# Values of the second block's attention made as channels by tokens, with four transposes in each layer

## The reference, cut to what matters

```python
h = modulate(rms_norm_2(x, norm_mix[l]), sh1, sc1)
hc = modulate(rms_norm_2(xc, norm_mix[l]), csh1, csc1)
k, v, q, u, f, gt = jnp.split(h @ w_in[l], IN_SPLITS, axis=-1)
if last:
    kc, vc = jnp.split(hc @ w_in[l][:, :2 * KV_WIDTH], 2, axis=-1)
else:
    kc, vc, qc, uc, fc, gtc = jnp.split(hc @ w_in[l], IN_SPLITS, axis=-1)
...
o = latent_attention(q, k, v, kc, vc, attn_sink[l])
...
o = (jnp.einsum('bhgnqk,bnkhd->bnqhgd', p_lat, vb)
     + jnp.einsum('bhgnqc,bchd->bnqhgd', p_ctx, vc))
```

## Time and profile before

| | us |
|---|---|
| median of three runs | 2189.99 |
| lowest, highest | 2189.62, 2190.36 |
| the profiled execution, its own time | 2188.52 |
| its span in the trace | 2186.8 |
| TensorE busy in the span | 2085.0 |
| VectorE, ScalarE, GpSimd busy | 1230.1, 1112.0, 959.3 |
| mean granted TensorE clock | 0.98 of full speed |

### The profile page before, as it was taken

The page is one execution under the profiler, slowest core; times in us unless marked ns, Lnnn a source line. Parts: engine busy times, 40 slices in busy tenths (PEclk is TensorE's granted clock), DMA queues, the critical chain, the costliest instruction groups (busy, mean ns, idle before and its releaser), DMA issues.

```text
span 2186.8 us, 36805 instructions
## 1 busy us (share of the span) xinstructions
PE 2085.0 (95%) x14870; PEld 1856.7 (85%) x14870; DVE 1230.1 (56%) x2034; ACT 1112.0 (51%) x1892; POOL 959.3 (44%) x424
## 2 busy tenths in 40 slices
PE   6999999999999999999999999999999989999997
PEld 6998998998898999988666876778888777898997
DVE  5577757345677655473464435455544546766565
ACT  5575476544585475554475233433333346645553
POOL 4655654653546555642112332323333233465662
PEclk9999999999999999999999999999999989999998
DMA  6454544565654544563212434333333333354551
GB/s 238 150 189 170 185 149 147 183 221 186 225 177 157 182 155 154 195 227 110 97 68 77 163 127 164 116 125 125 116 135 107 131 109 109 124 183 140 189 184 58
DMA packets 93321, 330.65 MB, mean 151 GB/s; under 512 B 10080, under 2 KB 13408, under 8 KB 92896
## 3 DMA queue, kind: packets, MB, share of 16 engines
q1 hardware_dynamic: 93152, 328.30, 43.6%
HBM read 327.08 MB, written 1.18 MB: 150 GB/s over the span
## 4 chain that ended last, share of the span: by engine, by line
PE 76%; DVE 11%; ACT 7%; issue 2%; DMA 2%; POOL 2%; SPq 0%; DVEq 0%; ACTq 0%; POOLq 0%
PE ps L878 21%; PE ps L879 21%; PE ps L880 21%; ACT t_hi L1239 2%; PE ps L932 2%; DVE t_lo L1554 1%; DMA t_A<-cu_scratch 1%; PE ps L891 1%; PE ps L892 1%; PE ps L893 1%; POOL t_lo L2021 1%; PE ps L1150 1%; DVE t_SQA L1564 1%; PE ps L1006 1%; PE ps L1160 1%
## 5 line engine op out<-in xcount | busy, mean ns | idle before, releaser
L2021 POOL TENSOR_TENSOR t_lo<-t_raw,t_hi 128x1024 fp32r<-128x1024 f32 (+1 forms) x360 | 884.9, 2468 | 1059.7 <-ACT t_hi L1239 1035.9
L878 PE MATMUL ps<-t_RB,t_hi 128*128 128x256 f32 (+1 forms) x3712 | 1170.8, 315 | 17.3 <-DVE t_RB L1842 5.3
L879 PE MATMUL ps<-t_RB,t_hi 128*128 128x256 f32 (+1 forms) x3712 | 1149.4, 310 | 0.0
L880 PE MATMUL ps<-t_RB,t_lo 128*128 128x256 f32 (+1 forms) x3712 | 1148.7, 309 | 0.0
L878 PEld LDWEIGHTS ps<-t_RB,t_hi 128*128 128x128 f32 x3712 | 712.3, 192 | 90.5 <-issue 31.5
L880 PEld LDWEIGHTS ps<-t_RB,t_lo 128*128 128x128 f32 x3712 | 712.6, 192 | 35.7
L879 PEld LDWEIGHTS ps<-t_RB,t_hi 128*128 128x128 f32 x3712 | 712.9, 192 | 34.9 <-issue 1.9
L1239 ACT ACTIVATE t_hi<-t_raw 128x1024 fp32r<-128x1024 f32 (+1 forms) x506 | 524.7, 1042 | 421.6 <-PE ps L880 387.9
L1554 DVE TENSOR_TENSOR t_lo<-t_raw,t_hi 128x1024 fp32r<-128x1024 f32 x146 | 211.2, 1447 | 264.4 <-ACT t_hi L1239 264.3
L1980 DVE SCALAR_TENSOR_TENSOR t_A<-ps,t_V,t_A 128x510 f32<-128x510 f32 (+1 forms) x176 | 102.2, 612 | 153.8 <-ACT t_A L1514 152.2
L1514 ACT ACTIVATE t_A<-ps,t_V 128x512 f32<-128x512 f32 (+1 forms) x88 | 48.5, 576 | 126.8 <-PE ps L880 126.8
(11 more groups left out here) (295 smaller groups left out, 2154.5 us busy)
## 6 DMA issues: line engine op xcount, KB each, us to landing
t_raw<-in_W SPq DMA_DIRECT2D x586, 512.0 KB, 3.5
t_A<-cu_scratch SPq DMA_DIRECT2D x8, 512.0 KB, 6.3
t_B<-cu_scratch SPq DMA_DIRECT2D x8, 512.0 KB, 4.4
t_raw<-in_W SPq DMA_DIRECT2D x16, 256.0 KB, 2.6
t_A<-in_C SPq DMA_DIRECT2D x2, 1536.0 KB, 6.8
t_X<-in_X SPq DMA_DIRECT2D x2, 512.0 KB, 4.4
t_X<-in_X SPq DMA_DIRECT2D x1, 1024.0 KB, 9.6
out<-t_X SPq DMA_DIRECT2D x1, 1024.0 KB, 4.8
```

The costliest lines, as they stand in the source:

```text
L878: mm(o, hi[:, w], xh(k), start=k == 0 and j == 0, stop=False)
L879: mm(o, hi[:, w], xl(k), start=False, stop=False)
L880: i = mm(o, lo[:, w], xh(k), start=False, stop=k == nkt - 1 and m == u.x[1] - 1)
L2021: tt(t.lo[s][:, 0:w], t.raw[r][:, 0:w], t.hi[s][:, 0:w].bitcast(F), ALU.subtract).then_inc(*up("pool", ("split", u.i)))
```

## The change

`v2` becomes a copy of `k2` on weight columns 128 to 255: the weight is stationary and 512 tokens stream past it, 24 matmuls in a layer. The result lies as channels by tokens. ScalarE copies it to `VR`, 512 columns in the constants' tile `C1` that no longer hold constants in use. One tick later than the one behind `v2`, a new unit `v2t` turns it: TensorE transposes four blocks of 128 by 128 into one of the small PSUM banks, and ScalarE copies this bank into `V2`. The waits of `pair4` are the same.

```diff
@@ block2
         self.add("v2", l=l, i=i, g=(self.bank(),))
         self.split_after(i, 1)
+        self.v2_turn(l)
         self.tick()
...
+    def v2_turn(self, l):
+        def g():
+            yield
+            self.add("v2t", l=l, s=(self.sbank(),))
+        self.side.append(g())
@@ Tiles
+        self.VR = self.C1[:, CONST["swap1"][0] + 512:CONST["swap1"][0] + 1024]
@@ tensor
     def v2(u):
-        toks(u, 8, 256, 128, 128, block(t.H2), block(t.HL2), (0, 1, 2, 3), lambda k: at("h", 3 + 2 * u.l, k), 1)
+        b, (xh, xl) = gbank(u), h2(512)
+        for k in range(8):
+            q.wait_ge(at("h", 3 + 2 * u.l, k))
+            hi, lo = weights(u, k, 256)
+            o = by_stream(b[:, :])
+            mm(o, hi[:, 128:256], xh(k), start=k == 0, stop=False)
+            mm(o, hi[:, 128:256], xl(k), start=False, stop=False)
+            i = mm(o, lo[:, 128:256], xh(k), start=False, stop=k == 7)
+            taken(u, i, k, 8, 256, ("mm", u.i, 1))
+
+    def v2t(u):
+        q.wait_ge(at("v2raw", u.l))
+        b = sbank(u)
+        for n in range(4):
+            i = e.transpose(b[:, n * 128:(n + 1) * 128], t.VR[:, n * 128:(n + 1) * 128], t.ident)
+        i.then_inc(*up("pe", ("v2tr", u.l)))
@@ scalar
     def v2(u):
-        act(t.V2[:, :, :], gbank(u, 1)[:, :].rearrange("p (b c) -> p b c", b=4), ACT.Copy).then_inc(
-            *up("act", ("v2", u.l), ("gfree", u.g[0])))
+        act(t.VR, gbank(u, 1)[:, :], ACT.Copy).then_inc(*up("act", ("v2raw", u.l), ("gfree", u.g[0])))
+
+    def v2t(u):
+        q.wait_ge(at("v2tr", u.l))
+        act(t.V2[:, :, :], t.sb[u.s[0] % 4][:, :].rearrange("p (b c) -> p b c", b=4), ACT.Copy).then_inc(
+            *up("act", ("v2", u.l), ("sfree", u.s[0])))
```

More of the change, by code:

```diff
@@ L1197, in tensor @@
                 small=small, small4=small4, vc=vc, vb=vc, scores=scores, turn=turn, pv=pv, ssm0=ssm0, ssm3=ssm3, ssm4=ssm4,
-                rope2=rope2, gn_sum=gn_sum, proj=proj, wout=wout, uf=uf, k2=k2, v2=v2, q2=lambda u: of_h2(u, 256 if u.l else 512),
+                rope2=rope2, gn_sum=gn_sum, proj=proj, wout=wout, uf=uf, k2=k2, v2=v2, v2t=v2t, q2=lambda u: of_h2(u, 256 if u.l else 512),
                 gate2=lambda u: of_h2(u, u.x[3]), rope2b=rope2b, pool1=pool1, four1=four1, mix2=mix2, pair0=pair0, pair3=pair3,
@@ L1529, in scalar @@
                 small1=small1, small2=small2, exp=exp, turn=turn, pv=pv, ssm0=ssm0, ssm1=ssm1, ssm3=ssm3, z=z, ysplit=ysplit,
-                gate=gate, gn_sum=gn_sum, gn_sqrt=gn_sqrt, msplit=msplit, rope=rope, norm2=norm2, uf=uf, mix2=mix2, k2=k2, v2=v2,
+                gate=gate, gn_sum=gn_sum, gn_sqrt=gn_sqrt, msplit=msplit, rope=rope, norm2=norm2, uf=uf, mix2=mix2, k2=k2, v2=v2, v2t=v2t,
                 q2=q2, pair1=pair1, pair3=pair3, pair4=pair4, gate2=gate2, msplit2=msplit2, up=ffup, glu=glu)
```

## The result

The changed kernel takes 2180.67 us (median of six runs, 2178.18 to 2183.98), the kernel before 2190.18 us beside it (six runs, 2189.46 to 2191.46); the ratio is 0.9957, with a 95% interval of 0.9944 to 0.997. A later comparison of the same two kernels gave 0.9967 (0.9955 to 0.9979). Over all comparisons together, 11 runs of the changed kernel have a mean of 2181.2 us and 53 runs of the kernel before one of 2189.4 us: 8.2 us less, give or take 1.3. The forecast was 2180.7 us, 9.3 less. That median and forecast agree to 0.03 us is luck, since single runs of the kernel before lie up to 6 us from their median; what the steps were worth has to be read from stretches of the traces.

A forecast was written before the change was run, and what follows sets the result against it. TensorE, busy for 95% of the span, was taken as the bound. 21.71 us removed, less 11.34 for the new products and 1.12 for transposes, gave 9.25 us less: median 2180.7 us, range 2177 to 2185.

The forecast's parts named there:

- The removed product: The old value products on TensorE, 10.85 us in layer 0 and 10.86 in layer 1, go: together 21.71 us.
- The new product: On TensorE, 24 matmuls of 512 columns, 0.228 us apart as for the keys: 5.67 us a layer, 11.34 in both.
- The transposes: Four float32 transposes a layer on TensorE add 0.56 us, 1.12 in both layers; bounds 0.51 and 1.09.
- The waits: The query product covers ScalarE's 0.60 us copy before the transposes; ScalarE's added copy falls into idle time; both cost nothing.
- The weights: Weight halves are given back sooner; in layer 1 at least 13 us of 16 stay in hand.
- The sum: Whole kernel: 21.71 − 11.34 − 1.12 = 9.25 us less, a median of 2180.7 us.
- a wait takes the place of the gain: Rival: late transposes or weight halves make TensorE stand, 2.3 us in each layer, about 2185.3 to 2190 us; chance 0.05.
- transposes let the clock fall: Slower rival: lower clock through layer 0's three query products, 14.4 us lost against 9.25 won, 2195.1 us; chance 0.03.
- the granted clock is dealt anew: Rival: clock falls behind the change differ; fewer give 2177.1 to 2178.9 us (0.12), more 2182.5 to 2186.1 (0.13).
- low stretches of the clock that change by more than 4 us in sum: Sign of being wrong: TensorE's stretches at a low granted clock change by more than 4 us in sum.
- The price of one fall: In layer 0's attention pairs, one clock fall slows nine 512-column matmuls by 0.20 us each: 1.8 us.

The follow-up runs named there:

- layer 1 alone: The kernel before with only layer 1 of the second block changed, layer 0 keeping its 96 matmuls of 128 columns: 2182.54 us, ratio 0.9966.
- transposes at once: The changed kernel with the transposes directly behind the value product, so the query product doesn't cover ScalarE's copy: 2183.65 us, ratio 0.9974.

## Why the prediction was right

- **The removed product** was read from its own rows, 10.85 and 10.86 us, and is gone.
- **The new product** was put at 5.67 us and took 5.66 and 5.68. Two errors cancel in it: the first distance behind the float32 group is 0.42 us, not 0.33 as in the earlier trace rows, and the last one 0.23, not 0.32 as in the earlier trace rows. The 22 distances in between are the 0.228 of the keys, the row on which the step rested.
- **The transposes** were put at 0.56 us in each layer, with 0.51 and 1.09 as bounds. The group took 0.49, just below the lower bound, and its net price was 0.40, by the trace without transposes, since the swap behind it starts the next product 0.09 us sooner than behind a branch step; the trace with eight times as many gives 0.11 for each further one. This is the one term that was sized wrong, by 0.16 us in each layer: the prediction added the group's own length and left its neighbour as it was.
- **The waits.** TensorE doesn't stand before the transposes. Without the query product as cover it stands 0.69 us, and the stretch grows by 0.91 to 0.96, where the prediction had 0.6. On ScalarE, the timeline answers the earlier trace rows: the copy into the values' tile (1486) ends at 1034.51, and the next high part starts at 1036.51 after 2.00 us of waiting for TensorE, as before.

```profile
1020.94 0.60 ACT L1482 ACTIVATE t_C<-ps 128x512 f32<-128x512 f32 x1 [1.60 <-PE ps L1112]
...
1033.93 0.58 ACT L1486 ACTIVATE t_A<-ps 128x512 f32<-128x512 f32 x1
1036.51 1.06 ACT L1262 ACTIVATE t_hi<-t_raw 128x1024 fp32r<-128x1024 f32 x1 [2.00 <-PE ps L888]
```

- **The weights.** In layer 1 the low part that answers the earlier trace rows now starts at 1788.34 and is ready at 1790.72; the first half of the second query chunk is given back at 1804.52, so 13.8 us are in hand, where 13 were forecast.

```profile
1788.34 2.38 POOL L2048 TENSOR_TENSOR t_lo<-t_raw,t_hi 128x1024 fp32r<-128x1024 f32 x1 [6.54 <-ACT t_hi L1262]
```

```profile
1804.52 1.06 ACT L1262 ACTIVATE t_hi<-t_raw 128x1024 fp32r<-128x1024 f32 x1 [2.96 <-PE ps L888]
```

- **The sum.** 9.25 us were forecast, and 4.84 and 4.81 us, together 9.65, found. Of the 0.40 us more, 0.32 are the net price of the transposes, 0.40 instead of 0.56 in each layer (in layer 1 the swap went from 0.78 us, 1809.27 to 1810.05, to 0.68, 1800.52 to 1801.20). Another 0.06 are the modulation's transposes behind the product, at 0.53 instead of 0.56 us (1020.74 to 1021.27) and 0.52 instead of 0.55 (1789.67 to 1790.19). That leaves 0.02. The pairs of both layers, the 614 us between the layers and the 316 us at the end kept their length to within what two traces of one kernel differ by, so nothing was given back. The last step of the sum took the median of three runs, 2189.99 us, as the base; over 53 runs the mean is 2189.4, and 9.65 less would be 2179.7, 1.0 below the forecast. The changed kernel's 11 runs have a mean of 2181.2, so the 8.2 us of the totals, give or take 1.3, fall just short of the 9.65 of the stretches. Totals miss their stretches both ways here (layer 1 alone won 7.5 by the medians and 4.8 by the stretch, transposes at once 6.1 and 7.8), which the scatter of the clock before the change can explain; for these runs, of which only one each has a trace, it isn't shown.
- **The rivals.** That a wait takes the place of the gain: refuted by the rows above. That transposes let the clock fall: refuted by the kernel with 32 of them in a layer. That the granted clock is dealt anew: it is, and it was underrated. The prediction took it for a consequence of the shift and argued from three runs 0.74 us apart that it comes out the same each time. In 53 runs the kernel before reached from 2183.95 to 2194.16 us. It isn't the change that deals it anew but every execution, and mostly in code before the change. The range of 8 us around the forecast held the median; it would not have held every single run of a kernel that never changed. For the same reason one of the prediction's signs of being wrong, low stretches of the clock that change by more than 4 us in sum, can't tell a change of the kernel: up to the keys alone the two traces of the kernel before differ by 4.5 us. The price of one fall was right: the first trace of the kernel before has the one at 1140 to 1145, and its pairs are 97.3 us long instead of 95.7, where 1.8 us had been worked out.

## What to carry to other kernels

A matmul with its own weight load costs nearly the same with 128 and with 256 streamed columns here, so a product with 128 is worth turning until it streams 256 or more, even at the price of transposes: 96 matmuls became 24, 10.85 us became 5.66, and four transposes took 0.40 back. A later step that is small itself can still cost by taking a place in a round of buffers: the same four transposes were free in the idle time with a bank of the other round, and cost 0.6 and 0.9 us in the pairs with a bank of the round that the pairs use. Where the effect is below the scatter of runs, compare stretches between two fixed instructions: here they repeated to 0.1 us while whole runs scattered by up to 6.

## What the runs showed of the hardware

- A transpose of 128 by 128 float32 in a row of others costs 0.11 us, though each record lasts 0.27; 32 of them took 3.55 us at a granted clock of 1.00.
- The first distance behind a float32 group depends on what the group ends with: 0.33 us behind the branch steps, 0.42 behind the rotary swap (1015.08 to 1015.50), and 0.31 for 256 columns behind the same swap (1011.04 to 1011.35).
- What stands in front of a group changes the price of that group: the rotary swap takes 0.34 us to the next product behind a branch step of 64*64 (1030.84 to 1031.18), 0.25 behind transposes of 128*128 (1033.05 to 1033.30), and 0.25 behind a branch step of 128*128 in the kernel before (1053.61 to 1053.86).
- The granted clock falls in one execution and not in the next, at the same instruction: in seven of twelve traces, after idle times of TensorE of 2.02 to 3.27 us, and not in five, after 2.45 to 2.89. The twelve traces, of kernels that are alike up to there, have their first key matmul between 1003.3 and 1010.7 us.
